# A hybrid decoder step: token tiles transposed by products with a diagonal of row scales, and the first loads reordered

## The chip, the core and the metric

The kernel runs on one core of a Trainium2 chip. The metric is the device time of one execution in microseconds (us), read as the median of the runs shown. TensorE (PE in the profile) multiplies, VectorE (DVE), ScalarE (ACT) and GpSimd (POOL) do the element-wise work, and SyncE (SP) issues most of the DMA transfers. Each engine works through its own list in order and meets the others at semaphores.

## The reference

One step of a decoder layer over 1072 token rows of width 1024: 32 sample tokens, 16 learned meta tokens and 1024 prompt tokens.

```
xn = x * rsqrt(mean(x * x) + eps) * norm_mix          # per token, all float32
z  = xn @ w_in                                        # 1024 -> 3592 columns
...                                                   # short convolutions, gated delta rule with state
h  = x + concat(y_a, y_b) @ w_out
h  = h + relu(rmsnorm(h) @ w_up)^2 @ w_down
y  = rmsnorm(h)                                       # meta tokens dropped from y_prompt
```

Only the first line, and the start of the second, are touched by the change.

## The kernel before

The kernel keeps activations with the features on the 128 partitions and the tokens along the free dimension. x arrives with tokens on the partitions, in nine tiles: tile 0 has 48 rows (samples and meta tokens, `x_small`), tiles 1 to 8 have 128 prompt rows each (`x_big`). The three **groups** of tokens (`GROUPS`) are tiles 0 to 2 (304 columns), tiles 3 to 5 and tiles 6 to 8 (384 columns each). The feature dimension is eight slices k of 128.

A float32 product with enough accuracy is made of three products in a faster type (float32r): high part of the weights by high part of xn, high by low, and low by high. So each 128-column weight tile n of `w_in` is split into `w_h` and `w_l`, and xn into `xh` and `xl`. `dense_part` (lines 1401 to 1403) issues the three products for one slice k of one group. `w_in` has 28 such tiles, and they are followed by `w_out`, `w_up` and `w_down`; TensorE works on them to the end of the kernel.

**How xn is made**, for a tile t:

1. SP loads it (lines 606 to 609 and 742 to 744; semaphores `s_xin`). In SP's list stand tile 0 in two parts, tile 1, tile 2, the first weight tile (line 619), the small block `ab_raw` of eight columns of `w_in` (line 741), tile 3, tiles 4 and 5 in one transfer, tiles 6 to 8 in one transfer. Then SP waits for tiles 4 and 5 and issues seven small loads.
2. ACT squares it and sums along the row (`square_x`, line 1022).
3. DVE makes the mean and adds eps (`mean_x`, line 2035).
4. POOL raises it to the power -1/2 (`x_power`, line 813), which gives `rx`.
5. DVE multiplies the whole tile by `rx` in place (`scale_x`, line 2041, semaphore `x_scaled`).
6. PE transposes the eight slices of it into PSUM banks against the identity `eye` (line 1440 for group 0, `turn_x`, line 1425, for groups 1 and 2). A bank holds one slice k of one group, so it is full when the last tile of the group has been transposed.
7. For each of the 24 pairs m = 8 g + k, ACT writes `xh` from the bank with the factor `tn` (norm_mix, line 1042), and DVE writes `xl` (line 2057).
8. PE waits for `x_low` of m and issues the three products of weight tile 0 (`dense_part(0, ...)`).

PE's list in this part is: the transpose of the norm rows; for each of the tiles 0, 1, 2 first some **idle products** (`IDLE_PRODUCTS`, 3, 1 and 1 of them, line 1431, whose result nobody reads) and then the eight transposes; a wait for `w_low`; the products of m = 0 to 7; `made_ab(0)`, sixteen products with the 16-column `ab_w` (lines 1452 and 1454), which wait for `ab_lo`; the transposes of m = 8 to 11; and then for each m from 8 to 23 the products of m and, five ahead, the transposes of m + 5. At m = 8 it also waits for `ab_kept` and transposes m = 12.

ACT's list is: squares of tiles 0, 1, 2, `split_high(0)` (the high part of weight tile 0, line 1015), the high part of `ab_raw` (line 1035), the square of tile 3, then the 24 evictions with the squares of tiles 4 to 8 between them (`SQUARE_AFTER`: tiles 4, 5, 6 after m = 7, tile 7 after m = 8, tile 8 after m = 10).

DVE's list is: for tiles 0, 1, 2 `mean_x` and `scale_x`; the low part of weight tile 0 (line 2050), `mean_x(3)`, then the 24 `xl` with the other `mean_x` and `scale_x` between them. POOL's list is the nine `x_power` with the low part of `ab_raw` (line 828) after the third. Both the idle products and the wait sit in these lines:

```
for t in GTILES[0]:
    idle_products(IDLE_PRODUCTS[t])
    if t == 0:
        pe.wait_ge(rows_kept, 1)
    pe.wait_ge(x_scaled, t + 1)
```

Of the kernel before, what the change touches and what calls it, by code (L numbers as in the profile page):

```python
# [7 lines left out]
ALU = mybir.AluOpType  # L8
ACT = mybir.ActivationFunctionType
AX = mybir.AxisListType  # L10
F32 = mybir.dt.float32
F32R = mybir.dt.float32r

P = 128
# [10 lines left out]
NT = 1 + SEQ // P  # L25
# [75 lines left out]
def build(nc, x_prompt, x_sample, state_conv_a, state_conv_qkv, state_ssm, meta_tokens, norm_mix, w_in,  # L101
# [4 lines left out]
    with ctx:  # L106
        NY, NSQ = 5, 6

        SLOT = TOK * 4
        R1 = 16512  # L110
        RK = R1 + 16 * SLOT
# [9 lines left out]
        def place(name, shape, dt, offset):  # L121
            return nc.alloc_sbuf_tensor_at(name, shape, dt, offset=offset)
# [10 lines left out]
        def sem(name):  # L133
            return ctx.enter_context(nc.semaphore(name))

        ps_pair = [ctx.enter_context(nc.psum_tensor(f"banks{i}", [P, 2, 512], F32)) for i in range(4)]
        ps = [ps_pair[i // 2][:, i % 2, :] for i in range(8)]
# [16 lines left out]
        w_raw = [place(f"w_raw{i}", [P, KT, P], F32, RING + 4096 * i) for i in range(2)]  # L154
# [7 lines left out]
        x_small = place("x_tok0", [P, D], F32, RZ)  # L162
        square_out = place("square_out", [P, D], F32, RK)
        rows_q = place("rows_q", [28, QKVW], F32, RG)
        rows_a = place("rows_a", [19, CONV], F32, RG + 6144)
        rows_n = place("rows_n", [16, P], F32, RG + 8192)
        ab_raw = place("ab_raw", [P, KT, 8], F32, RG + 3 * SLOT)
# [145 lines left out]
        O_BANK, S_BANK, L_BANK, M_BANK = 4, 5, 6, 7  # L313

        s_norm = sem("s_norm"); s_row = sem("s_row"); s_xin = [sem(f"s_xin{i}") for i in range(6)]; s_const = sem("s_const")
        x_sq = sem("x_sq"); x_pow = sem("x_pow"); x_ms = sem("x_ms"); x_scaled = sem("x_scaled")
        x_turned = sem("x_turned"); x_high = sem("x_high"); x_low = sem("x_low")
        set_ones = sem("set_ones"); rows_turned = sem("rows_turned"); rows_kept = sem("rows_kept")
        ab_hi = sem("ab_hi"); ab_lo = sem("ab_lo"); ab_made = sem("ab_made"); ab_kept = sem("ab_kept")
# [194 lines left out]
        def x_tile(t):  # L514
            return x_small[0:C0, :] if t == 0 else x_big[:, t - 1, :]
# [8 lines left out]

        SQUARE_AFTER = {7: (4, 5, 6), 8: (7,), 10: (8,)}
        AB_AFTER = 9
        IDLE_PRODUCTS = (3, 1, 1)
        TURN_AHEAD = 5

        def turn_bank(g, k):  # L530

            m = KT * g + k
            return k if g == 0 else 3 + (m - KT) % 5

        def rows(t):
            return C0 if t == 0 else P
# [67 lines left out]
        def _(sp):  # L604
# [2 lines left out]
            sp.dma_start(x_small[NS:C0, :], meta_tokens).then_inc(s_xin[0], 16)  # L607
            sp.dma_start(x_big[:, 0:1, :], xp_v[:, 0:1, :]).then_inc(s_xin[1], 16)
            sp.dma_start(x_big[:, 1:2, :], xp_v[:, 1:2, :]).then_inc(s_xin[2], 16)

            def load(n):
                if n >= 2:
# [122 lines left out]
            for n in range(N_IN + 3):  # L735
                if n >= 3:
                    step(3 * (n - 3))
                    step(3 * (n - 3) + 1)
                load(n)
                if n == 0:  # L740
                    sp.dma_start(ab_raw[:, :, :], w_in_v[:, :, O_A:O_A + 8]).then_inc(s_ahead, 16)
                    sp.dma_start(x_big[:, 2:3, :], xp_v[:, 2:3, :]).then_inc(s_xin[3], 16)
                    sp.dma_start(x_big[:, 3:5, :], xp_v[:, 3:5, :]).then_inc(s_xin[4], 16)
                    sp.dma_start(x_big[:, 5:8, :], xp_v[:, 5:8, :]).then_inc(s_xin[5], 16)
                    sp.wait_ge(s_xin[4], 16)
                    sp.dma_start(rows_q[0:24, :], state_conv_qkv.rearrange("l b r c -> (l b r) c")).then_inc(s_row, 16)
                    sp.dma_start(rows_q[24:28, :], conv_qkv_w[0]).then_inc(s_row, 16)
                    sp.dma_start(rows_a[0:16, :], state_conv_a.rearrange("l b r c -> (l b r) c")).then_inc(s_row, 16)
                    sp.dma_start(rows_a[16:19, :], conv_a_w[0]).then_inc(s_row, 16)
                    sp.dma_start(gn[:, :], gdn_norm.rearrange("l (p a) -> (l p) a", a=1)).then_inc(s_row, 16)  # L750
                    sp.dma_start(al[:, :], a_log.to_broadcast([P, NH])).then_inc(s_row, 16)
                    sp.dma_start(dtb[:, :], dt_bias.to_broadcast([P, NH])).then_inc(s_row, 16)
                if n >= 3:
                    step(3 * (n - 3) + 2)
# [50 lines left out]
        def _(pool):  # L805
# [17 lines left out]

            for t in range(NT):
                x_power(t)
                if t == 2:
                    pool.wait_ge(ab_hi, 1)
                    pool.tensor_tensor(ab_w[:, :, 8:16], ab_raw[:, :, :], ab_w[:, :, 0:8].bitcast(F32),
                                       ALU.subtract).then_inc(ab_lo, 1)
# [176 lines left out]
        def _(act):  # L1006
# [3 lines left out]
            def split_high(n):  # L1010

                act.wait_ge(w_load[n % 2], 16 * (n // 2 + 1))
                if n >= 2:
                    act.wait_ge(acc_done, 3 * (n - 1))
                act.activation(w_h[n % 2][:, :, :], w_raw[n % 2][:, :, :], ACT.Copy).then_inc(w_high, 1)  # L1015
# [14 lines left out]

            for t in GTILES[0]:
                square_x(t)
            split_high(0)
            act.wait_ge(s_ahead, 16)
            act.activation(ab_w[:, :, 0:8], ab_raw[:, :, :], ACT.Copy).then_inc(ab_hi, 1)
            square_x(3)
            act.wait_ge(rows_kept, 1)
            for m in range(3 * KT):
                g, k = m // KT, m % KT
                c0, w = GROUPS[g]  # L1040
                act.wait_ge(x_turned, m + 1)
                act.activation(xh[:, k, c0:c0 + w], ps[turn_bank(g, k)][:, 0:w], ACT.Copy,
                               scale=tn[:, k:k + 1]).then_inc(x_high, 1)
                for t in SQUARE_AFTER.get(m, ()):
                    square_x(t)
                if m == AB_AFTER:
                    keep_ab(0)
# [346 lines left out]
        def _(pe):  # L1394
# [21 lines left out]
            def turn_x(m):  # L1416

                g, k = m // KT, m % KT
                c0 = GROUPS[g][0]
                pe.wait_ge(x_low, m - 4 if m >= KT + 5 else m - KT + 4)  # L1420
                for t in GTILES[g]:
                    o, c = tile_cols(t)
                    if k == 0:
                        pe.wait_ge(x_scaled, t + 1)
                    ins = pe.transpose(ps[turn_bank(g, k)][:, o - c0:o - c0 + c], x_tile(t)[:, P * k:P * k + P],
                                       eye[0:c, 0:c])
                ins.then_inc(x_turned, 1)

            def idle_products(count):
# [3 lines left out]
            for t in GTILES[0]:  # L1433
                idle_products(IDLE_PRODUCTS[t])
                if t == 0:
                    pe.wait_ge(rows_kept, 1)
                pe.wait_ge(x_scaled, t + 1)
                o, c = tile_cols(t)
                for k in range(KT):
                    ins = pe.transpose(ps[turn_bank(0, k)][:, o:o + c], x_tile(t)[:, P * k:P * k + P], eye[0:c, 0:c])  # L1440
                    if t == GTILES[0][-1]:
                        ins.then_inc(x_turned, 1)

# [579 lines left out]
        def _(dve):  # L2023
# [8 lines left out]
            def mean_x(t):  # L2032

                dve.wait_ge(x_sq, t + 1)
                dve.tensor_scalar(ssx[0:rows(t), t:t + 1], ssx[0:rows(t), t:t + 1], 1.0 / D, EPS, ALU.mult,
                                  ALU.add).then_inc(x_ms, 1)

            def scale_x(t):

                dve.wait_ge(x_pow, t + 1)  # L2040
                dve.tensor_scalar(x_tile(t), x_tile(t), rx[0:rows(t), t:t + 1], None, ALU.mult).then_inc(x_scaled, 1)

            for t in GTILES[0]:
                mean_x(t)
                if t == 0:
                    dve.wait_ge(rows_turned, 1)
                    dve.tensor_copy(tn[:, :], ps[0][:, 0:16]).then_inc(rows_kept, 1)
                scale_x(t)
            dve.wait_ge(w_high, 1)
            dve.tensor_tensor(w_l[0][:, :, :], w_raw[0][:, :, :], w_h[0][:, :, :].bitcast(F32),  # L2050
                              ALU.subtract).then_inc(w_low, 1)
            mean_x(3)
            for m in range(3 * KT):
                g, k = m // KT, m % KT
                c0, w = GROUPS[g]
                dve.wait_ge(x_high, m + 1)
                dve.scalar_tensor_tensor(out=xl[:, k, c0:c0 + w], in0=ps[turn_bank(g, k)][:, 0:w], scalar=tn[:, k:k + 1],  # L2057
                                         in1=xh[:, k, c0:c0 + w].bitcast(F32), op0=ALU.mult,
                                         op1=ALU.subtract).then_inc(x_low, 1)
                if m == KT - 1:  # L2060
                    scale_x(3)
                    mean_x(4)
                    mean_x(5)
                    scale_x(4)
                    scale_x(5)
                    mean_x(6)
                if m == KT:
                    scale_x(6)
                    mean_x(7)
                if m == KT + 2:  # L2070
                    scale_x(7)
                    mean_x(8)
                if m == KT + 3:
                    scale_x(8)
            dve.wait_ge(rows_turned, 2)
            dve.tensor_copy(tq[:, :, :], ps[3][:, 0:336].rearrange("p (f r) -> p f r", r=28)).then_inc(rows_kept, 1)
            dve.tensor_copy(ta[:, :, :], ps[4][:, 0:76].rearrange("p (f r) -> p f r", r=19)).then_inc(rows_kept, 1)
# [704 lines left out]
```

## Time and profile before

| | us |
|---|---|
| three runs | 1331.97, 1333.32, 1335.27 |
| their median | 1333.32 |
| the profiled execution, its own time | 1332.77 |
| its span, first to last instruction | 1331.0 |
| PE busy with products | 1314.0 (99%) |
| DVE, POOL, ACT busy | 840.4, 524.3, 412.7 |

The span lies inside the execution's own time; 1.8 us are outside it. In the timeline a row gives start, duration, engine, line, operation and how many were merged. PE matmuls are pipelined, so the durations overlap: the pace is the distance between starts. A float32 product shows as two records of PE, a float32r product and a transpose as one. PEld is the load of the stationary operand, which runs beside the products.

### The profile page before, as it was taken

How to read it: one execution, taken by the hardware profiler on the slowest of the kernel's cores; microseconds unless marked ns; L12 is line 12 of the kernel's file. 1: busy time of each engine (PE TensorE's matmuls, PEld its weight loads, DVE VectorE, ACT ScalarE, POOL GpSimd, SP SyncE). 2: the span in 40 equal slices, each digit the busy share in tenths (PEclk: the TensorE clock that was granted, in tenths of full speed). 3: DMA queues.
4: the chain of work that ended last, by engine and by line, in shares of the span. 5: the costliest groups of instructions: out<-in, count | busy, mean ns of one | idle time of the engine just before them, and what ended most of it. 6: DMA issues, size and time to landing. Idle time of an engine off the chain costs nothing.

```text
span 1331.0 us, 22484 instructions
## 1 busy us (share of the span) xinstructions
PE 1314.0 (99%) x8988; PEld 1282.5 (96%) x8988; DVE 840.4 (63%) x1414; ACT 412.7 (31%) x807; POOL 524.3 (39%) x544
## 2 busy tenths in 40 slices
PE   7999999999999999999999999999999999999997
PEld 6899999899999999999999999999999999999997
DVE  6566898436463665556666756756667567566866
ACT  7566652112221213232122222322222223222313
POOL 2322112111111211221367466574574755746811
PEclk9999999999999999999999999999999999999999
DMA  6223553633323323221111212112011121110213
GB/s 193 62 73 91 163 166 80 194 115 88 88 65 82 101 57 90 81 65 48 48 33 48 64 33 63 33 48 64 33 61 51 36 61 48 49 49 32 80 45 118
DMA packets 161947, 99.88 MB, mean 75 GB/s; under 512 B 19736, under 2 KB 156468, under 8 KB 161843
## 3 DMA queue, kind: packets, MB, share of 16 engines
q1 hardware_dynamic: 138866, 85.56, 21.9%
q10 hardware_dynamic: 22976, 12.88, 3.6%
q8 instruction: 72, 1.18, 0.4%
q14 instruction: 33, 0.26, 0.1%
HBM read 77.62 MB, written 20.80 MB: 74 GB/s over the span
## 4 chain that ended last, share of the span: by engine, by line
PE 93%; DVE 3%; ACT 2%; issue 1%; DMA 1%; SPq 0%; POOL 0%; DVEq 0%; ACTq 0%
PE banks L1401 10%; PE banks L1927 9%; PE banks L1403 9%; PE banks L1402 9%; PE banks L1929 9%; PE banks L1928 9%; PE banks L1946 7%; PE banks L1947 7%; PE banks L1945 7%; PE banks L1963 1%; PE banks L1964 1%; PE banks L1965 1%; PE banks L1621 1%; PE banks L1635 1%; PE banks L1857 1%
## 5 line engine op out<-in xcount | busy, mean ns | idle before, releaser
L1927 PE MATMUL banks<-hg_high,w_high 128*128 128x384 f32 (+1 forms) x768 | 249.5, 325 | 0.0
L1929 PE MATMUL banks<-hg_high,w_low 128*128 128x384 f32 (+1 forms) x768 | 247.6, 322 | 0.0
L1928 PE MATMUL banks<-hg_low,w_high 128*128 128x384 f32 (+1 forms) x768 | 247.3, 322 | 0.0
L2674 DVE TENSOR_TENSOR hT<-hT,banks 128x528 f32<-128x528 f32 x280 | 189.4, 701 | 84.0 <-PE banks L1947 76.0
L1401 PE MATMUL banks<-xn_high,w_high 128*128 128x384 f32 (+1 forms) x672 | 226.8, 337 | 0.6 <-DVE xn_low L2057 0.5
L1403 PE MATMUL banks<-xn_high,w_low 128*128 128x384 f32 (+1 forms) x672 | 218.1, 325 | 0.0
L1402 PE MATMUL banks<-xn_low,w_high 128*128 128x384 f32 (+1 forms) x672 | 218.0, 324 | 0.0
L821 POOL TENSOR_TENSOR w_low<-w_raw,w_high 128x1024 fp32r<-128x1024 f32 x31 | 77.0, 2483 | 243.7 <-ACT w_high L1015 243.7
L1927 PEld LDWEIGHTS banks<-hg_high,w_high 128*128 128x128 f32 x768 | 144.2, 188 | 1.9 <-POOL w_low L947 1.7
L1928 PEld LDWEIGHTS banks<-hg_low,w_high 128*128 128x128 f32 x768 | 144.3, 188 | 0.1
L1929 PEld LDWEIGHTS banks<-hg_high,w_low 128*128 128x128 f32 x768 | 144.2, 188 | 0.0
L966 POOL TENSOR_TENSOR w_low<-w_pair,w_high 128x256 fp32r<-128x256 f32 x140 | 104.0, 759 | 66.4 <-ACT w_high L1334 66.4
L2653 DVE TENSOR_TENSOR u_row<-banks,h_squares 128x384 f32<-128x384 f32 (+1 forms) x96 | 50.1, 522 | 126.4 <-PE banks L1929 126.1
L1401 PEld LDWEIGHTS banks<-xn_high,w_high 128*128 128x128 f32 x672 | 126.5, 188 | 3.1 <-DVE xn_low L2057 1.1
L947 POOL TENSOR_TENSOR w_low<-w_raw,w_high 128x1024 fp32r<-128x1024 f32 x31 | 78.3, 2527 | 126.9 <-ACT w_high L1316 120.7
L1947 PE MATMUL banks<-op_high_T,w_low 128*128 128x264 f32 x448 | 127.7, 285 | 0.0
L1946 PE MATMUL banks<-op_low_T,w_high 128*128 128x264 f32 x448 | 127.7, 285 | 0.0
L1945 PE MATMUL banks<-op_high_T,w_high 128*128 128x264 f32 x448 | 127.1, 284 | 0.0
L1402 PEld LDWEIGHTS banks<-xn_low,w_high 128*128 128x128 f32 x672 | 126.7, 189 | 0.0
L1403 PEld LDWEIGHTS banks<-xn_high,w_low 128*128 128x128 f32 x672 | 126.2, 188 | 0.0
L1334 ACT ACTIVATE w_high<-w_pair 128x256 fp32r<-128x256 f32 x140 | 55.4, 415 | 177.6 <-PE banks L1929 84.3
L1947 PE MATMUL banks<-op_high_B,w_low 128*128 128x264 f32 x336 | 95.8, 285 | 0.0
(333 smaller groups left out, 2783.6 us busy)
## 6 DMA issues: line engine op xcount, KB each, us to landing
w_raw<-in_w_up SPq DMA_DIRECT2D x32, 512.0 KB, 4.0
w_pair<-in_w_down SPq DMA_DIRECT2D x32, 512.0 KB, 3.4
w_raw<-in_w_in SPq DMA_DIRECT2D x28, 512.0 KB, 4.3
w_raw<-in_w_out SPq DMA_DIRECT2D x8, 512.0 KB, 4.1
x_slice<-in_x_prompt SPq DMA_DIRECT2D x8, 512.0 KB, 4.2
out<-y_tok SPq DMA_DIRECT2D x8, 512.0 KB, 2.7
v_kept_rows<-v_feat SPq DMA_DIRECT2D x4, 536.0 KB, 2.9
gate_kept_rows<-gate_row SPq DMA_DIRECT2D x4, 536.0 KB, 3.1
```

The source lines that it names most:

```text
L947: pool.tensor_tensor(w_l[half][:, :, :], w_raw[n % 2][:, :, :], w_h[half][:, :, :].bitcast(F32), ALU.subtract).then_inc(w_low, 1)
L966: pool.tensor_tensor(set_of(w_l, b, s), set_source(n, PRODUCTS[x][0]), set_of(w_h, b, s).bitcast(F32), ALU.subtract).then_inc(w_low, 1)
L1401: pe.matmul(bank[:, 0:w], w_h[n % 2][:, k, :], hi[:, c0:c0 + w], start=(k == first), stop=False)
L1402: pe.matmul(bank[:, 0:w], w_h[n % 2][:, k, :], lo[:, c0:c0 + w], start=False, stop=False)
L1403: ins = pe.matmul(bank[:, 0:w], w_l[n % 2][:, k, :], hi[:, c0:c0 + w], start=False, stop=(k == last))
L1927: pe.matmul(bank[:, 0:w], w_h[half][:, k, :], hg_h[:, k, c0:c0 + w], start=(k == 0), stop=False)
L1928: pe.matmul(bank[:, 0:w], w_h[half][:, k, :], hg_l[:, k, c0:c0 + w], start=False, stop=False)
L1929: ins = pe.matmul(bank[:, 0:w], w_l[half][:, k, :], hg_h[:, k, c0:c0 + w], start=False, stop=(k == KT - 1))
L1945: pe.matmul(bank, high[:, j, :], op_h[name][:, j, cols], start=(j == 0), stop=False)
L1946: pe.matmul(bank, high[:, j, :], op_l[name][:, j, cols], start=False, stop=False)
L1947: ins = pe.matmul(bank, low[:, j, :], op_h[name][:, j, cols], start=False, stop=(j == FB // 2 - 1))
L2674: dve.tensor_tensor(hc, hc, both, ALU.add if sign > 0 else ALU.subtract).then_inc(acc_read_dve, 1)
```

## The change

The tiles of x are no longer scaled. For each tile DVE makes instead a diagonal matrix `x_root[t]`, the identity times `rx`, of 48 x 48 or 128 x 128. PE then multiplies each slice of the tile with this matrix, as an ordinary float32 product, where it transposed against `eye` before. The bank holds the same values as before. The load of tile 3 is moved ahead of the first weight tile in SP's list. The high part of weight tile 0 is made by DVE and no longer by ACT. The high part of `ab_raw` moves in ACT's list from before the square of tile 3 to behind the eviction of m = 3, and its low part on POOL from behind the third `x_power` to behind the fourth. `mean_x(3)` moves ahead of the split of weight tile 0. The idle products ahead of tiles 1 and 2 are dropped.

```
+        x_root = [place(f"x_root{t}", [P, P], F32, RK + 16 * SLOT + 4 * P * t) for t in range(NT)]
...
-        IDLE_PRODUCTS = (3, 1, 1)
+        IDLE_PRODUCTS = (3, 0, 0)
...
             sp.dma_start(x_big[:, 1:2, :], xp_v[:, 1:2, :]).then_inc(s_xin[2], 16)
+            sp.dma_start(x_big[:, 2:3, :], xp_v[:, 2:3, :]).then_inc(s_xin[3], 16)
...
                     sp.dma_start(ab_raw[:, :, :], w_in_v[:, :, O_A:O_A + 8]).then_inc(s_ahead, 16)
-                    sp.dma_start(x_big[:, 2:3, :], xp_v[:, 2:3, :]).then_inc(s_xin[3], 16)
...
                 x_power(t)
-                if t == 2:
+                if t == 3:
                     pool.wait_ge(ab_hi, 1)
...
             for t in GTILES[0]:
                 square_x(t)
-            split_high(0)
-            act.wait_ge(s_ahead, 16)
-            act.activation(ab_w[:, :, 0:8], ab_raw[:, :, :], ACT.Copy).then_inc(ab_hi, 1)
             square_x(3)
             act.wait_ge(rows_kept, 1)
             for m in range(3 * KT):
...
+                if m == 3:
+                    act.wait_ge(s_ahead, 16)
+                    act.activation(ab_w[:, :, 0:8], ab_raw[:, :, :], ACT.Copy).then_inc(ab_hi, 1)
...
-                        pe.wait_ge(x_scaled, t + 1)
-                    ins = pe.transpose(ps[turn_bank(g, k)][:, o - c0:o - c0 + c], x_tile(t)[:, P * k:P * k + P],
-                                       eye[0:c, 0:c])
+                        pe.wait_ge(x_rooted, t + 1)
+                    ins = pe.matmul(ps[turn_bank(g, k)][:, o - c0:o - c0 + c], x_tile(t)[:, P * k:P * k + P],
+                                    x_root[t][0:c, 0:c], start=True, stop=True)
...
-                dve.tensor_scalar(x_tile(t), x_tile(t), rx[0:rows(t), t:t + 1], None, ALU.mult).then_inc(x_scaled, 1)
+                dve.tensor_scalar(x_root[t][0:c, 0:c], eye[0:c, 0:c], rx[0:c, t:t + 1], None, ALU.mult).then_inc(x_rooted, 1)
...
-                scale_x(t)
+                root_x(t)
+            mean_x(3)
+            dve.wait_ge(w_load[0], 16)
+            dve.tensor_copy(w_h[0][:, :, :], w_raw[0][:, :, :]).then_inc(w_high, 1)
             dve.wait_ge(w_high, 1)
             dve.tensor_tensor(w_l[0][:, :, :], w_raw[0][:, :, :], w_h[0][:, :, :].bitcast(F32),
                               ALU.subtract).then_inc(w_low, 1)
-            mean_x(3)
```

The transposes of group 0 (line 1440) are replaced in the same way, and the other calls of `scale_x` become `root_x` at the same places.

## Rows read from the trace of the kernel before

**Rows 1.** The page: busy time of the engines, and shares of the chain that ended last.

```profile
PE 1314.0 (99%) x8988; PEld 1282.5 (96%) x8988; DVE 840.4 (63%) x1414; ACT 412.7 (31%) x807; POOL 524.3 (39%) x544
...
PE 93%; DVE 3%; ACT 2%; issue 1%; DMA 1%; SPq 0%; POOL 0%; DVEq 0%; ACTq 0%
```

**Rows 2.** Timeline, PE alone: the end of this part.

```profile
36.03 0.34 PE L1403 MATMUL banks<-xn_high,w_low 128*128 128x384 f32 x1
```

**Rows 3.** Timeline, PE alone: idle products, transposes of group 0, first products.

```profile
5.62 2.45 PE L1431 MATMUL banks<-c_main 128*128 128x208 f32 x6
8.00 1.09 PE L1440 MATMUL banks<-c_main,x_tok 48*128 48x48 f32 x8
9.87 1.91 PE L1440 MATMUL banks<-c_main,x_tok 128*128 128x128 f32 x8
12.27 1.91 PE L1440 MATMUL banks<-c_main,x_tok 128*128 128x128 f32 x8
14.38 0.50 PE L1401 MATMUL banks<-xn_high,w_high 128*128 128x304 f32 x1 [0.20 <-DVE xn_low L2057]
14.72 0.30 PE L1402 MATMUL banks<-xn_low,w_high 128*128 128x304 f32 x1
17.93 1.26 PE L1452 MATMUL banks<-xn_high,ab_w 128*16 128x304 f32 x8
```

**Rows 4.** Timeline: ACT and DVE around the first weights and evictions.

```profile
8.14 1.06 ACT L1022 ACTIVATE square_out<-x_tok 128x1024 f32<-128x1024 f32 x1 [0.85 <-DMA x_tok<-in_x_prompt]
10.09 1.06 ACT L1015 ACTIVATE w_high<-w_raw 128x1024 fp32r<-128x1024 f32 x1 [0.79 <-DMA w_raw<-in_w_in]
11.18 1.23 DVE L2050 TENSOR_TENSOR w_low<-w_raw,w_high 128x1024 fp32r<-128x1024 f32 x1 [0.28 <-ACT w_high L1015]
12.11 1.06 ACT L1022 ACTIVATE square_out<-x_tok 128x1024 f32<-128x1024 f32 x1 [0.82 <-DMA x_tok<-in_x_prompt]
13.17 3.33 ACT L1042 ACTIVATE xn_high<-banks,tn 128x304 fp32r<-128x304 f32 x8
13.70 3.63 DVE L2057 SCALAR_TENSOR_TENSOR xn_low<-banks,tn,xn_high 128x304 fp32r<-128x304 f32 x8 [0.25 <-ACT xn_high L1042]
```

**Rows 5.** Timeline from the end of `made_ab(0)`: PE, and ACT's eviction and `abT`.

```profile
20.14 0.38 PE L1425 MATMUL banks<-c_main,x_tok 128*128 128x128 f32 x2
21.24 0.58 ACT L1042 ACTIVATE xn_high<-banks,tn 128x384 fp32r<-128x384 f32 x1 [0.70 <-PE banks L1425]
22.53 0.44 PE L1401 MATMUL banks<-xn_high,w_high 128*128 128x384 f32 x1 [0.34 <-DVE xn_low L2057]
23.22 0.40 ACT L1029 ACTIVATE abT<-banks 16x304 f32<-16x304 f32 x1
23.67 0.87 PE L1425 MATMUL banks<-c_main,x_tok 128*128 128x128 f32 x6 [0.35 <-ACT abT L1029]
```

**Rows 6.** The chain that ended last, window 0 to 80: one m of its steady part.

```profile
31.52 0.18 PE banks L1403
31.70 0.33 PE banks L1425 x3
```

**Rows 7.** The chain in other windows (100 to 300): groups of four float32 products, 128 columns.

```profile
245.94 1.09 PE banks L1621 x8
281.15 0.89 PE banks L1656 x8
```

**Rows 8.** Groups by line and form, DVE: the nearest rows to what DVE gets.

```profile
L2041 DVE TENSOR_SCALAR x_tok<-x_tok,rx 128x1024 f32<-128x1024 f32 x8 | 6.0, 747 | 1.8 <-POOL rx L813 1.8
L2315 DVE COPY blocks<-inverse 128x1024 f32<-128x1024 f32 x1 | 1.1, 1127 | 0.0
```

**Rows 9.** One stretch of 1 us: busy time (x instructions) by engine, granted clock, DMA share, GB/s.

```profile
10.00:11.00 1.00, 1.00 (x7) 1.00 (x6) 0.75 (x1) 0.92 (x1) 0.11 (x1) 1.00 0.97 389
```

**Rows 10.** Timeline of SP's queue (issue start and duration), and POOL's low part of `ab_raw`.

```profile
3.69 4.41 SPq L742 DMA_DIRECT2D x_tok<-in_x_prompt  x1
14.66 0.37 SPq L746 DMA_DIRECT2D rows_q<-in_state_conv_qkv  x1
...
11.37 1.22 POOL L828 TENSOR_TENSOR ab_w<-ab_raw,ab_w 128x64 fp32r<-128x64 f32 x1 [1.25 <-ACT ab_w L1035]
```

More of the change, by code:

```diff
@@ L315, in build @@
         s_norm = sem("s_norm"); s_row = sem("s_row"); s_xin = [sem(f"s_xin{i}") for i in range(6)]; s_const = sem("s_const")
-        x_sq = sem("x_sq"); x_pow = sem("x_pow"); x_ms = sem("x_ms"); x_scaled = sem("x_scaled")
+        x_sq = sem("x_sq"); x_pow = sem("x_pow"); x_ms = sem("x_ms"); x_rooted = sem("x_rooted")
         x_turned = sem("x_turned"); x_high = sem("x_high"); x_low = sem("x_low")
@@ L1436, in _ @@
                     pe.wait_ge(rows_kept, 1)
-                pe.wait_ge(x_scaled, t + 1)
+                pe.wait_ge(x_rooted, t + 1)
                 o, c = tile_cols(t)
                 for k in range(KT):
-                    ins = pe.transpose(ps[turn_bank(0, k)][:, o:o + c], x_tile(t)[:, P * k:P * k + P], eye[0:c, 0:c])
+                    ins = pe.matmul(ps[turn_bank(0, k)][:, o:o + c], x_tile(t)[:, P * k:P * k + P], x_root[t][0:c, 0:c],
+                                    start=True, stop=True)
                     if t == GTILES[0][-1]:
@@ L2036, in mean_x, with root_x @@
                                   ALU.add).then_inc(x_ms, 1)
-            def scale_x(t):
+            def root_x(t):
+                c = rows(t)
                 dve.wait_ge(x_pow, t + 1)
-                dve.tensor_scalar(x_tile(t), x_tile(t), rx[0:rows(t), t:t + 1], None, ALU.mult).then_inc(x_scaled, 1)
+                dve.tensor_scalar(x_root[t][0:c, 0:c], eye[0:c, 0:c], rx[0:c, t:t + 1], None, ALU.mult).then_inc(x_rooted, 1)
             for t in GTILES[0]:
@@ L2060, in _ @@
                 if m == KT - 1:
-                    scale_x(3)
+                    root_x(3)
                     mean_x(4)
                     mean_x(5)
-                    scale_x(4)
-                    scale_x(5)
+                    root_x(4)
+                    root_x(5)
                     mean_x(6)
                 if m == KT:
-                    scale_x(6)
+                    root_x(6)
                     mean_x(7)
                 if m == KT + 2:
-                    scale_x(7)
+                    root_x(7)
                     mean_x(8)
                 if m == KT + 3:
-                    scale_x(8)
+                    root_x(8)
             dve.wait_ge(rows_turned, 2)
```

## The prediction

> **What bounds the kernel now.** I read the page first. TensorE is busy for 1314.0 of 1331.0 us and holds 93% of the chain that ended last [rows 1]. So work added to PE lengthens the kernel unless it fits into one of PE's waits. The timeline of the first 40 us shows what ends last there. The reader should look for three stretches. Up to 14.38 PE runs idle products and the transposes of group 0 and then waits for the first `xl` [rows 3]. From 14.38 to 20.14 it runs the products of m = 0 to 7 and `made_ab(0)`, closely packed [rows 3, 5]. From 20.14 to about 27.5 it still waits in places, for `xl` and for `abT` among others [rows 5]; from there to 36.37 it never waits, and each m costs three products and three transposes [rows 2, 6]. Behind 36.37 the work on PE is the same in both kernels, so the shift of that moment is the answer.
>
> **PE's added work.** In the steady part three transposes hold 0.33 us of the chain, 0.11 each [rows 6]. A float32 product of the same shape is two records: eight records, which are four products, hold 0.89 [rows 7], 0.223 a product. Each of the 48 turned slices of groups 1 and 2 thus costs 0.112 more, 5.4 us in all. Nothing else of the change lowers PE's work in that stretch.
>
> What of it goes into waits: from 20.14 to 36.37 are 16.2 us. The work in them is 48 transposes at 0.111, 5.3, and the products of m = 8 to 23, 48 at 0.175 (0.18 in the chain's rounding [rows 6]), 8.4, together 13.7. So PE waited 2.5 us. Afterwards the work is 48 x 0.223 + 8.4 = 19.1. The waits go because PE is then later than its suppliers: an m costs it 0.525 + 0.67 = 1.2 us, while an eviction costs ACT or DVE about 0.6. One wait may be left. The turning of m = 12 needs `abT`, and ACT makes that behind the eviction of m = 8, the square of tile 7 and the eviction of m = 9; from the first to the end of `abT` were 2.4 us before, less what it waited between (21.24 to 23.62 [rows 5]). With the turning of m = 8 done at 21.0 that gives 23.4, and with a signal's way 23.5; PE arrives at 20.1 + 12 x 0.223 + 0.525 = 23.3: 0.2 lost. The stretch becomes 19.3 and the change of it **+3.1 us**.
>
> **The start, to 20.14.** Three things must be there before the products of m = 0.
> (1) The weights. The transfer of tile 3 (524 KB) is now ahead of them. At the 389 GB/s of that time [rows 9] it takes 1.35 us, so they land at 10.1 + 1.35 = 11.45; if they and tile 3 simply change places, at 12.1 [rows 4]. DVE's copy is not in the trace. Its neighbours are the scaling of a tile of the same size from SBUF, 0.747, and a copy of the same size with turned strides, 1.127 [rows 8]. I take 0.75, since both sides are contiguous as in the scaling, and keep 1.13 for the range. The low part is 1.23 [rows 4]. That makes 11.45 + 0.75 + 1.25 = 13.45 for `w_low`, and DVE starts `xl` of m = 0 at 13.5 where it started at 13.70. Bounds: 13.2 (weights 0.3 earlier) to 14.6 (12.1, slow copy).
> (2) The banks. `x_high` started at 13.17 because ACT was still squaring tile 3, which landed at 12.1 [rows 4]. Now tile 3 follows tile 2, whose square began at 8.14 [rows 4], by 1.35; ACT is free at 10.8 and follows PE. The scaling of 0.75 becomes a 128 x 128 one; between a tiny one of about 0.15 and 0.747 [rows 8] I take 0.2, a gain of 0.5 for each tile, but PE, not DVE, is last here.
> (3) PE's own list. It is ready for tile 0 at 8.0 as before [rows 3]. The transposes of tiles 1 and 2 go at (1.91 - 0.42) / 7 = 0.213 a record [rows 3], twice the 0.111 of later [rows 6]. The granted clock reads 1.00 here too [rows 9], yet this pace is that of 1.2 GHz and the later one that of 2.4 GHz; the fast pace sets in at 14.7, right after the first weight product [rows 3]. The products take for tile 0 sixteen records at 0.11, 1.8 us (0.9 before), and for tiles 1 and 2 sixteen each: 3.4 us a tile at the slow pace, 1.8 at the fast one. Dropped are two idle products, 1.4 us. With the slow pace for tile 1 and the fast one for tile 2 the list is done at 8.0 + 1.8 + 3.4 + 1.8 = 15.0; with the fast pace from the middle of tile 1 at 14.1.
> The products of m = 0 to 7 then end at 18.3 in the first case (15.0 + 8 x 0.42) and at 17.6 in the second, where DVE's pace of 0.45 an m from 13.5 binds; 17.93 before [rows 3]. I take **0** for the start, with -0.4 and +2.3 as ends.
>
> The Trainium skill ("TensorE: Matmul & The Clock Gate", PE-mode transpose) says that transposes do not count as TensorE work for releasing its clock. By that rule the root products, which are ordinary ones, would bring the fast pace earlier than transposes did. The trace agrees as far as it goes: the slow pace outlasts 24 transposes. The sum stays the same by it, since `w_low` binds then; by the rule alone the first rival would have a smaller chance than the rows give it.
>
> **What is moved.** On SP the weights and `ab_raw` are issued one issue of 0.44 later. The issue that stood for 4.41 us, as behind a full queue [rows 10], will be that of `ab_raw` or of tiles 4 and 5; those landed at 14.6, where SP goes on [rows 10], and ACT takes them up behind m = 7, after 16.3, so 1.7 us cover it. The seven small loads behind are read after 36 [rows 2]. On ACT 1.06 for the weights goes, and the high part of `ab_raw` (0.24) comes behind m = 3, about 14.5; the evictions behind it run ahead of DVE's `xl`, so it costs nothing. On POOL the low part (1.22 [rows 10]) then ends at about 16.0. `made_ab(0)` waits for it at 17.9, and queued behind it is the power of tile 4, which wants a square that ACT makes only behind m = 7, after 17: over 1 us of cover for both. On DVE the split now waits for the weights with the 24 `xl` queued behind it; that is in (1). From m = 8 on the root steps take 0.5 less each than the scalings, on an engine that is no longer last there: nothing.
>
> **Sum.** 0 + 3.1 = +3.1 us. The profiled execution took 1332.77, so 1335.9 against its own time; the median of the three runs, 1333.32, is 0.55 higher, so 1336.4 beside it, or +0.23%. What a measurement of this kernel can tell from no change is about 0.3%, 4 us, so this counts as no change, close to the border.
>
> **Rivals.**
> *The clock stays slow through tiles 1 and 2* (slower). Both tiles take 3.4 us, so PE is done with tile 2 at 8.0 + 1.8 + 6.8 = 16.6, the products of m = 0 to 7 end at 20.1, 2.2 later than before, and the total is +5.3, 1338.6. For it: about 9 us of idle products and transposes did not bring the fast pace before. Against it: PE now runs products without a gap from 5.6 on, where it had transposes between. It decides slower once the slow pace reaches 1 us into tile 2's work. Chance 0.16.
> *Each bunch of products pays for a held weight load* (slower). Eight records behind a wait held 1.09 instead of 0.89 in one place [rows 7]. The 16 bunches of `turn_x` each stand behind a wait; 16 x 0.2 = 3.2 more, +6.3 in all, 1339.6. Against it: the transposes have the same waits and show no such loss [rows 6]. Chance 0.06.
> *The weights come late* (no change or slower). Landing at 12.1 and a copy of 1.13: `xl` starts 0.9 later than before, total +4.0, 1337.3. Chance 0.10.
> *A product with the root matrix costs a transpose's time.* Then the change doesn't add PE work, the scalings leave DVE, and half of PE's 2.5 us of waits and a little of the start are won: -1.5, 1331.8. Against it stand all float32 products of the trace. Chance 0.08.
> *Forecast*, its own range 1335.3 to 1337.5: chance 0.60.
>
> **Chances.** Slower by over 0.3%: 0.16 + 0.06 + half of 0.10 + about a tenth of the forecast's 0.60 (its upper end lies at the border), 0.33. Faster: a part of the last rival, 0.03. The rest, 0.64, is no change. The range takes in the forecast, the late weights and the slow clock, and above it half a microsecond for the spread of runs: up to 1339.2. Below it reaches to no change at all, 1333.3, where half of what the last rival wins is met. Left out are the second rival and the lower half of the last, about 0.1.
>
> **What would show it.** Right: the last three-product row of m = 23 near 39.5 instead of 36.0; the rows of the turning twice as many and 0.67 us for each three; no waits of PE behind 24; the first products of weight tile 0 near 14.2 to 15. Wrong: turning records at 0.21 apart for tile 2 (first rival), more than 1.3 us from one m to the next (second), DVE's low part of the weights ending after 14 (third), one record for each turned slice (fourth). The forecast falls as a whole if the span changes by less than 1.5 or more than 5 us.

## The result and the profile after

| | before | after |
|---|---|---|
| median of six runs each, us | 1333.17 | 1340.81 |
| lowest and highest of the changed kernel | | 1338.61, 1342.40 |
| ratio, 95% interval | | 1.0050 [1.0039, 1.0061] |
| profiled execution, its own time | 1332.77 | 1342.40 |
| its span | 1331.0 | 1340.6 |

The changed kernel is slower by 0.50%, 6.7 us (1333.2 x 0.0050). The forecast was +3.1 us, 1336.4, and the range ended at 1339.2: the sign was right and the size under half. The whole interval lies above the 0.3% up to which the prediction counted a shift as no change (0.64 of its chances); this is the case to which it gave 0.33. The page of the kernel after, busy time and shares of the chain, answers to [rows 1]:

```profile
PE 1324.5 (99%) x9056; PEld 1295.2 (97%) x9056; DVE 835.9 (62%) x1415; ACT 412.4 (31%) x806; POOL 523.8 (39%) x544
...
PE 95%; DVE 3%; ACT 1%; issue 1%; DMA 0%; ACTq 0%; DVEq 0%
```

PE gained work, DVE and ACT lost a little, and PE's share of the chain rose. The next view is the timeline of PE alone in the kernel after, from its first instruction to the end of m = 23; it answers to [rows 2, 3, 5].

```profile
6.32 0.25 PE L1411 MATMUL banks<-c_main,rows_n 16*128 16x16 f32 x1 [6.32 <-DMA rows_n<-in_norm_ffn]
6.50 2.45 PE L1432 MATMUL banks<-c_main 128*128 128x208 f32 x6
8.88 9.84 PE L1441 MATMUL banks<-x_root,x_tok 48*128 48x48 f32 x48
18.47 0.38 PE L1402 MATMUL banks<-xn_high,w_high 128*128 128x304 f32 x1
...
21.88 1.27 PE L1454 MATMUL banks<-xn_high,ab_w 128*16 128x304 f32 x8
...
24.10 2.84 PE L1426 MATMUL banks<-x_root,x_tok 128*128 128x128 f32 x24
...
43.23 0.34 PE L1404 MATMUL banks<-xn_high,w_low 128*128 128x384 f32 x1
```

The reader is to see one unbroken row of 48 root records where before there were three bunches of eight transposes with idle products between [rows 3], and two shifts:

| stretch | before | after | difference |
|---|---|---|---|
| start of the turning of tile 0 | 8.00 | 8.88 | +0.9 |
| from there to the first weight product | 6.38 | 9.59 | +3.2 |
| m = 0 to 7 | 3.55 | 3.41 | -0.1 |
| `made_ab(0)` | 2.21 | 2.22 | 0 |
| from there to the last product of m = 23 | 15.89 | 19.13 | +3.2 |
| last product of m = 23 | 36.03 | 43.23 | +7.2 |

The first 0.9 belongs to the execution, not to the change: PE's first instruction waits for a load (`rows_n`), and in the three runs below that have the same load order it starts at 4.80 to 4.97. So 6.3 us are the change's own.

How the start spends its time, in the groups by form of PE between 8.8 and 17.3 in the kernel after, then between 7.9 and 14.3 in the kernel before:

```profile
L1441 PE MATMUL banks<-x_root,x_tok 128*128 128x128 f32 x22 | 5.1, 428 | 0.0
L1441 PE MATMUL banks<-x_root,x_tok 48*128 48x48 f32 x16 | 3.6, 412 | 0.0
```

```profile
L1440 PE MATMUL banks<-c_main,x_tok 128*128 128x128 f32 x16 | 3.8, 421 | 0.0
...
L1440 PE MATMUL banks<-c_main,x_tok 48*128 48x48 f32 x8 | 1.1, 308 | 0.0
```

Durations overlap, so the price of a transpose is read from its starts: the last seven transposes of tile 0 start between 8.14 and 8.78 in the kernel before, 0.11 us apart, half of the 0.21 of a large tile. A root record of tile 0 took 3.6 / 16 = 0.22, the same as one of a large tile (5.1 / 22 = 0.23; from start to start both are 0.21). Sixteen records at 0.22 are 3.5 us, not the 1.8 of the forecast. Windows over the same row, of line L1441 alone (busy PE with its records, busy PEld, granted clock, DMA share, GB/s):

```profile
8.80:12.40 3.60, 3.52 (x16) 3.49 (x16) 1.00 1.16 297
12.40:15.40 3.00, 3.00 (x15) 2.95 (x15) 1.00 1.02 399
17.00:17.50 0.50, 0.50 (x4) 0.50 (x4) 1.00 1.02 406
17.50:18.00 0.50, 0.50 (x7) 0.50 (x6) 1.00 1.10 226
```

A window also counts a record that reaches over its edge. Four records in half a microsecond are the slow pace, seven the fast one: it comes only at 17.5, when tile 2 is half done. The granted clock reads 1.00 throughout, as it did before at this pace [rows 9], so in these records the start's level has to be read from the pace.

What ACT and DVE did in the meantime, in the timelines of ACT and DVE, answering to [rows 4]:

```profile
16.76 1.73 ACT L1040 ACTIVATE xn_high<-banks,tn 128x304 fp32r<-128x304 f32 x4 [6.00 <-PE banks L1441]
...
11.77 0.69 DVE L2054 CAST w_high<-w_raw 128x1024 fp32r<-128x1024 f32 x1 [0.82 <-DMA w_raw<-in_w_in]
12.49 1.23 DVE L2056 TENSOR_TENSOR w_low<-w_raw,w_high 128x1024 fp32r<-128x1024 f32 x1
17.30 3.63 DVE L2062 SCALAR_TENSOR_TENSOR xn_low<-banks,tn,xn_high 128x304 fp32r<-128x304 f32 x8 [3.58 <-ACT xn_high L1040]
```

ACT stood idle for 6.00 us and DVE for 3.58, both behind PE. The weights were split by 13.7, near the 13.45 of the forecast, and nobody waited for them. The steady part, one m of the chain that ended last and the start of the next (start, duration, what), answers to [rows 6]:

```profile
31.91 0.67 PE banks L1426 x6
32.58 0.18 PE banks L1402
32.76 0.17 PE banks L1403
32.93 0.18 PE banks L1404
33.11 0.67 PE banks L1426 x6
```

An m costs 33.11 - 31.91 = 1.20 us without a wait, as forecast (0.525 + 0.67).

Behind 43.23 the work is the same, and there one thing differs between executions: stretches at half clock. Windows of PE alone, first the kernel after, then before (busy time with records, granted clock, DMA share, GB/s):

```profile
65.00:69.00 4.00, 4.00 (x20) 0.57 0.04 12
249.00:253.50 4.50, 4.50 (x22) 0.62 0.46 137
```

```profile
65.00:69.00 4.00, 4.00 (x25) 1.00 0.49 131
249.00:253.50 4.50, 4.50 (x20) 1.00 0.39 118
```

A granted clock of 0.57 over 4 us is 3.4 us at half speed; so is 0.62 over 4.5. For work that is bound by the clock alone such a stretch would cost half of that, 1.7 us. What it did cost can be read behind the last product of m = 23: the rest of the span is 1294.3 and 1295.0 us in the profiled executions without one (e1 below, and before), 1295.8 to 1296.3 in those with one (e3, e4, e8) and 1297.3 to 1297.5 in those with two (after, e2, e5, e6, e7), so 1.2 to 1.5 us each. The two profiles differ by 9.6 us: 7.2 up to m = 23 and 2.4 behind it, where the medians differ by 7.6 and the paired ratio says 6.7.

The kernel before has such stretches in other runs: the mean granted clock runs from 0.995 to 0.998 in the changed kernel's runs and from 0.995 to 0.999 in the 62 runs of the kernel before whose clocks are on record. The changed kernel's run at 0.998 has a span of 1336.8, and the seventeen of the kernel before at 0.998 have a mean of 1330.8: 6.0 apart, near the 6.3 of the table above. Whether the change makes the stretches more frequent is open: four of its six runs are at 0.995, and eight of the 62.

### The profile page after: what moved, and what is told of

The parts are those of the page before. It is cut to its first block, busy times and chain, and to the rows that moved or that the text cites. A ratio compares the mean times of both kernels' runs of the same rounds, so it can differ in the third digit from the quotient of the medians.

```text
span 1340.6 us, 22620 instructions
## 1 busy us (share of the span) xinstructions
PE 1324.5 (99%) x9056; PEld 1295.2 (97%) x9056; DVE 835.9 (62%) x1415; ACT 412.4 (31%) x806; POOL 523.8 (39%) x544
## 4 chain that ended last, share of the span: by engine, by line
PE 95%; DVE 3%; ACT 1%; issue 1%; DMA 0%; ACTq 0%; DVEq 0%
PE banks L1402 10%; PE banks L1404 9%; PE banks L1403 9%; PE banks L1929 9%; PE banks L1931 9%; PE banks L1930 9%; PE banks L1948 7%; PE banks L1949 7%; PE banks L1947 7%; PE banks L1965 1%; PE banks L1966 1%; PE banks L1967 1%; PE banks L1623 1%; PE banks L1637 1%; PE banks L1426 1%
```

## The experiments

Eight kernels ran, in two sets of four, each against the kernel before on the same chip. **A** says that the time is PE's own added work, in group 0 and in groups 1 and 2; **B** that the moved load or the moved steps cost something; **C** that the half clock of the start doubles what the root products of group 0 cost.

| kernel | first weight product | last product of m = 23 | ratio to before, 95% interval |
|---|---|---|---|
| before | 14.38 | 36.03 | 1 |
| after | 18.47 | 43.23 | 1.0050 [1.0039, 1.0061] |
| e1, roots in group 0 alone | 17.10 | 38.28 | 1.0023 [1.0014, 1.0032] |
| e2, roots in groups 1 and 2 alone | 13.70 | 38.56 | 1.0021 [1.0012, 1.0030] |
| e3, no roots, the rest of the change | 14.00 | 35.81 | 1.0001 [0.9992, 1.0010] |
| e4, after, with dense products first | 14.34 | 39.21 | 1.0013 [1.0004, 1.0022] |
| e5, before, with dense products first | 13.44 | 35.06 | 1.0003 [0.9993, 1.0012] |
| e6, after, with the old load order | 16.40 | 41.27 | 1.0041 [1.0028, 1.0054] |
| e7, e3 with dense products first | 13.30 | 34.41 | 0.9996 [0.9986, 1.0005] |
| e8, e5 with a square moved | 12.49 | 34.90 | 0.9992 [0.9984, 1.0001] |

### One part at a time: e1, e2, e3

e1 keeps the root products of group 0 and turns groups 1 and 2 with transposes again, whose tiles DVE scales as before:

```
-  ins = pe.matmul(ps[turn_bank(g, k)][:, ...], x_tile(t)[:, ...], x_root[t][0:c, 0:c], start=True, stop=True)
+  ins = pe.transpose(ps[turn_bank(g, k)][:, ...], x_tile(t)[:, ...], eye[0:c, 0:c])
...
+  if t >= 3: dve.tensor_scalar(x_tile(t), x_tile(t), rx[0:c, t:t + 1], None, ALU.mult)
```

> The changed kernel with the tiles of groups 1 and 2 scaled and transposed as before (48 transposes in place of 48 root products); group 0, the loads and the split as changed. Theory A (PE's own work): each turned slice of groups 1 and 2 is one record of 0.11 us instead of two, 5.3 us less work of which 2 come back as waits, so about 3.2 us faster than the changed kernel, some 3.5 to 4 slower than the kernel before; the products of m = 0 start where they start in the changed kernel, 18.5. Theory B (the start alone, the load order and what hangs on it, makes the loss): no faster than the changed kernel by more than 1 us.

e2 is the reverse:

```
-  IDLE_PRODUCTS = (3, 0, 0)
+  IDLE_PRODUCTS = (3, 1, 1)
...
-  ins = pe.matmul(ps[turn_bank(0, k)][:, o:o + c], x_tile(t)[:, ...], x_root[t][0:c, 0:c],
+  ins = pe.transpose(ps[turn_bank(0, k)][:, o:o + c], x_tile(t)[:, ...], eye[0:c, 0:c])
...
+  if t < 3: dve.tensor_scalar(x_tile(t), x_tile(t), rx[0:c, t:t + 1], None, ALU.mult)
```

> The changed kernel with group 0 scaled and transposed as before, and the idle products back at 3, 1, 1; groups 1 and 2 with root products, loads and split as changed. Theory A: PE's list ahead of the first weight product shortens by the 24 doubled slices, 3.2 us, so the first weight product starts near 15.2 (14.4 plus 0.9 for the late first transfer) and the kernel is about 3.2 us faster than the changed one. Theory B (load order): the first weight product stays behind 17.5 and the gain is under 1 us. The row of m = 23's last product then stands near 40.

e3 makes both edits, so that of the change only the load order, the split on DVE and the moved steps (both parts of `ab_raw`, `mean_x(3)`) are left. The idle products ahead of tiles 1 and 2 go with group 0 in these edits; no run separates dropping them from the root products of that group.

> The changed kernel with all nine tiles scaled and transposed as before and the idle products at 3, 1, 1: what is left is the load order, DVE's high part of the weights and the moved parts of the small block. Theory A: within 1 us of the kernel before, 0.9 of it from the constants that land later (first PE instruction at 6.3 instead of 5.4). If the two root parts add up, its gain over the changed kernel is the sum of those of the two kernels that restore one part each, about 6.4 us. Theory B: still 3 us or more slower than the kernel before.

Measured: 1337.71, 1337.60 and 1335.06 beside 1334.59 of the kernel before. The parts are +0.23%, +0.21% and +0.01%, together 0.45% against 0.50% of the whole change; the intervals allow full additivity. The moves alone cost nothing (**B** falls), and each of the two sets of root products costs about 3 us (**A** stands). Inside the executions, from the first start of tile 0 to the last product of m = 23, it adds up as well: 28.0 us before, 30.9 in e1 (+2.8), 31.0 in e2 (+3.0), 28.2 in e3 (+0.2) and 34.4 after (+6.3). The stamps came 1.4 to 1.5 us sooner than expected in e1 and e2, since their expectations counted the changed kernel's late first load as a part of the load order. It is not: e1, e2 and e3 have that order and start at 4.85, 4.80 and 4.97. e1's timeline of PE has the same unbroken row as the changed kernel, 9.9 us of it, though it began 1.5 us sooner:

```profile
4.85 0.26 PE L1411 MATMUL banks<-c_main,rows_n 16*128 16x16 f32 x1 [4.85 <-DMA rows_n<-in_norm_ffn]
...
7.41 9.94 PE L1441 MATMUL banks<-x_root,x_tok 48*128 48x48 f32 x48
17.10 0.39 PE L1402 MATMUL banks<-xn_high,w_high 128*128 128x304 f32 x1
```

In e2 transposes and root products meet in one timeline of PE: in group 0 the transposes of tiles 0, 1 and 2, then the turning of m = 8 to 11.

```profile
4.80 0.25 PE L1411 MATMUL banks<-c_main,rows_n 16*128 16x16 f32 x1 [4.80 <-DMA rows_n<-in_norm_ffn]
...
7.57 1.06 PE L1441 MATMUL banks<-c_main,x_tok 48*128 48x48 f32 x8
...
9.50 1.97 PE L1441 MATMUL banks<-c_main,x_tok 128*128 128x128 f32 x8
...
11.95 1.32 PE L1441 MATMUL banks<-c_main,x_tok 128*128 128x128 f32 x8
...
19.43 2.84 PE L1426 MATMUL banks<-x_root,x_tok 128*128 128x128 f32 x24
```

Tile 2's eight transposes hold 1.32, against 1.97 for tile 1: here the fast pace came at about 12.5, early in tile 2 and 7.7 us after PE's first instruction, with nothing but transposes and idle products ahead of it. With root products it came after 11.2 us in the changed kernel (17.5 - 6.3), 11.4 in e1 (16.3, from where the starts of its records come 0.11 apart, less 4.85) and 9.8 in e6 below (14.7 - 4.93), with transposes after 9.3 in the kernel before (14.7 - 5.4) and 9.7 in e3. Root products did not bring it earlier than transposes. The Trainium skill ("TensorE: Matmul & The Clock Gate", PE-mode transpose) says that transposes do not count for releasing the clock. By that rule the root products should have brought the fast pace earlier, and in these few executions they did not; the rule itself is not tested, since idle products, which are ordinary ones, stand among the transposes. Why the slow pace outlasted some 40 root records without a gap stays open.

### The clock of the start: e4 and e5

Nine 512-column products on a tile of ones that nobody reads stand ahead of PE's first product; e4 has them in the changed kernel, e5 in the kernel before:

```
+  pool.memset(warm[:, :].bitcast(F32), 1.0).then_inc(set_ones, 1)
...
+  pe.wait_ge(set_ones, 1)
+  for _ in range(9):
+      pe.matmul(ps[7][:, 0:512], warm[:, 0:P], warm[:, 0:512], start=True, stop=True)
```

> The changed kernel with nine dense products of 512 columns on a constant tile put on PE ahead of its first wait (about 1.5 to 5.5 us, when PE was idle), nothing else. Theory C (the slow pace of the start is the clock's lower level, which PE's earlier work decides): the 48 records of group 0 go 0.11 apart instead of 0.213 and take 5.3 us instead of 9.6, the first weight product starts near 14.6 and the kernel is 3 to 4 us faster than the changed one. Rival D (the pace of 0.213 belongs to float32 products and transposes that start cold from DMA-fed tiles, whatever PE did before): the records stay 0.213 apart and the time does not change by more than 0.5 us.

> The kernel before with nine dense 512-column products ahead of its first product and nothing else changed. Theory A (the change lost time to TensorE's own work at half clock; the first stage of the kernel before has slack on TensorE, since ScalarE's first eviction waited for ScalarE's own list until 13.17): the start gains little, first weight product at 13.9 to 14.4 against 14.38, time 1333.5 to 1334.6 (0 to -0.8 us against the kernel before), so that the warm-up which was worth 4 us to the changed kernel is worth under 1 us here, and the changed kernel with it stays behind this one by about 2 to 3 us. Rival E (the half clock costs every kernel's start the same): the same 4 us gain here, 1330.5. A gain between 1.5 and 3 would say that the slack on TensorE is smaller than the chain shows.

Measured: 1336.37 (e4). Against the changed kernel 0.50% became 0.13%: 4.9 us came back (0.0037 x 1333; by the ends of the two intervals 2.3 to 7.6), where 3 to 4 were expected. By the stamp of m = 23, 3.2 us of loss are left (39.21 less 36.03), the price of groups 1 and 2; the ratio says 1.7, and its interval ends at 2.9. The timeline of PE in e4:

```profile
1.31 4.21 PE L1413 MATMUL banks<-warm 128*128 128x512 f32 x9 [1.31 <-POOL minus_half L810]
5.86 0.20 PE L1416 MATMUL banks<-c_main,rows_n 16*128 16x16 f32 x1 [0.34 <-DMA rows_n<-in_norm_ffn]
5.99 1.32 PE L1437 MATMUL banks<-c_main 128*128 128x208 f32 x6
7.24 7.34 PE L1446 MATMUL banks<-x_root,x_tok 48*128 48x48 f32 x48
14.34 0.38 PE L1404 MATMUL banks<-xn_high,w_high 128*128 128x304 f32 x1
```

The six idle products take 1.32 instead of 2.45 [rows 3]. The windows of the root row in e4 (columns as above) show both levels in one row, and here the granted clock tells them apart:

```profile
7.20:9.00 1.80, 1.76 (x15) 1.76 (x16) 0.95 1.03 365
9.00:12.00 3.00, 3.00 (x15) 2.91 (x15) 0.50 0.99 256
12.00:14.40 2.40, 2.40 (x22) 2.39 (x21) 0.95 1.03 420
```

At the fast level a record of the 48-row tile takes 0.12 (1.80 / 15) and one of a large tile 0.11; at half clock it is 0.20. So a root record's price halves with the clock and does not depend on whether the tile has 48 or 128 columns: **C** stands, and tile 0's 3.5 us is explained. PE did stay dense between 9 and 12, yet the clock fell back for that time, so the row took 7.34 and not the 5.3 expected. In e5 and e8, which have transposes there and PE busy for 2.5 and 2.6 of the same 3 us, it did not fall. Why is not settled, and whether more dense work would hold it was not tried.

e5: 1334.68, against 1333.77 for the kernel before in its set; no gain. Its first weight product comes 0.9 sooner than before, 13.44, twice what was expected of it at most, since the square of tile 3 on ACT also happened to begin 0.9 sooner (its DMA was done earlier in this execution). The timeline of ACT in e5 shows what the first eviction waits for, a square and not PE:

```profile
11.17 1.06 ACT L1024 ACTIVATE square_out<-x_tok 128x1024 f32<-128x1024 f32 x1 [0.21 <-DMA x_tok<-in_x_prompt]
...
12.23 3.33 ACT L1044 ACTIVATE xn_high<-banks,tn 128x304 fp32r<-128x304 f32 x8
```

The rival that the half clock costs every kernel alike (1330.5) falls. With transposes the half clock is hidden behind ACT's list but for about 1 us; with root products nothing hides it. That the earlier end of m = 23 (35.06) does not show in the median goes with more time at half clock in e5's runs: five of its twelve have a mean granted clock of 0.994, which no run of the kernel before has. At equal mean clock (0.995, 0.996, 0.997, 0.998) e5's mean span is shorter than that of the kernel before in its set by 0.6, 1.6, 1.0 and 1.8 us, from few runs each. Whether the dense products bring the extra time at half clock is open.

### The load order with root products: e6

```
-  sp.dma_start(x_big[:, 2:3, :], xp_v[:, 2:3, :])        # ahead of load(0)
...
+  sp.dma_start(x_big[:, 2:3, :], xp_v[:, 2:3, :])        # behind ab_raw, as before
```

> The changed kernel with the load of the third large tile put back behind the weights and ab_raw; root products everywhere. Theory A (TensorE's own work): 1340 +- 1.5 like the changed kernel, root products of the start at 0.21 us per record until about 17, first weight product 18 to 18.7. Rival B (the moved load costs something of its own): 1337.5 or less, with the first weight product 1.5 us or more sooner than 18.47.

Measured: 1339.83 against 1333.77, ratio 1.0041, which overlaps the changed kernel's. **A** is right on the time: **B** wanted 1337.5 or less. The stamps missed: the first weight product came at 16.40, not 18 to 18.7. PE's first instruction was early (4.93 where the changed kernel's was at 6.32), and from the start of tile 0 the root row took 8.90 instead of 9.59, since the fast pace came at 14.7, 7.2 us after that start, where the changed kernel had it after 8.6 (17.5 - 8.88). A stamp of one execution shifts by more than the median does; differences inside an execution are what can be compared.

### Is there a version that beats both: e7 and e8

e7 is e3 with the dense products. e8 is e5 with the square of tile 3 off ACT's path to the first eviction:

```
-  square_x(3)                    # ahead of ACT's eviction loop
+  if m == 3: square_x(3)         # in it, behind the eviction of m = 3
...
-  mean_x(3)                      # ahead of DVE's xl loop
+  if m == 4: mean_x(3)           # in it, behind xl of m = 4
```

> Transposes everywhere with the new load order and VectorE's high part (the run without roots) and the nine dense products ahead. VectorE's chain there: tile 2 scaled at 11.2, high part to 11.95, low part to 13.2, first low part of x at 13.3 to 13.8. Theory A with VectorE as the bound of that start: first weight product 13.7 to 14.0, time 1334.3 to 1335.2, 0 to -0.6 us against the run without roots. If TensorE at half clock was still the bound there: first weight product 13.2, and 1 us less time.

> The kernel before with the nine dense products ahead, and with the square of the third large tile moved on ScalarE behind the eviction of m=3 (its mean on VectorE behind m=4). With both covers of the first eviction gone (ScalarE's square until 13.1, TensorE's half clock) it starts at about 12.2 instead of 13.17: first weight product 13.2 to 13.5, time 1333.2 to 1333.8 against about 1334.6 of the kernel before (-0.8 to -1.4 us). If only one of the two bounds the start, it equals the run with the dense products alone.

Measured: 1333.52 (e7) and 1333.08 (e8) against 1333.77. e7 did better than expected: its first weight product came at 13.30, not 13.7 to 14.0, and still behind a wait of 1.63 us for DVE, whose low part of the weights began 0.5 us sooner than in e3 (11.48 against 11.97). It also gives the pair for e4: with the dense products the changed kernel is 0.17% slower than its version without root products (1.0013 and 0.9996, from two sets), 2.3 us, and without them 0.49%, 6.5 us. e8's first weight product came sooner than its 13.2 to 13.5 too. ACT's timeline in e8:

```profile
10.55 0.24 ACT L1037 ACTIVATE ab_w<-ab_raw 128x64 fp32r<-128x64 f32 x1
10.98 1.73 ACT L1043 ACTIVATE xn_high<-banks,tn 128x304 fp32r<-128x304 f32 x4 [0.20 <-PE banks L1446]
12.59 1.07 ACT L1024 ACTIVATE square_out<-x_tok 128x1024 f32<-128x1024 f32 x1
```

With both covers gone the first eviction starts at 10.98, and the first weight product at 12.49, 1.9 us sooner than before. But the square now sits between two evictions, PE waits for `xl` of m = 4, and by the end of m = 23 only 1.1 us are left (34.90). The ratio is 0.9992 with an interval that reaches 1.0001: the estimate, -1.1 us (0.0008 x 1334), fits the expectation, but this many runs do not show it to be a gain. Neither version is shown to be faster than the kernel before; both beat the changed kernel.

## Why the prediction was wrong

- **PE's added work in groups 1 and 2**: right. The forecast was +3.1; measured are +3.24 in the stretch 20.14 to 36.03 of before against 24.10 to 43.23 of after, +2.8 us in e2's time (0.0021 x 1334). The 0.223 for a root product was right (0.67 for three), and so was the 1.20 of an m. The 0.2 of waiting for `abT` did not come: the stretch took 19.13, not 19.3.
- **The start**: wrong, and the failing step is (3), "PE's own list". "The products take for tile 0 sixteen records at 0.11, 1.8 us" took the pace of tile 0's transposes for the price of a root record. Measured: 0.22 a record, 3.5 us, so +1.7. At the half clock a transpose of the 48-row tile took half of a large tile's time; a float32 record of the same tile took as much as a large tile's. The second half of the step, the fast pace for all of tile 2, gave 1.8 where it took about 2.7 (eight records at 0.21, eight at 0.11, and a little to the first weight product): +0.9. And "I take **0** for the start" chose between +0.4 of the sum and -0.4: another 0.4. Together 3.0 of the 3.1 that the start really cost (17.93 to 21.88 less 0.88).
- **The range's end of +2.3** took in the slow clock and the late weights, but no row for tile 0's records; that is why it missed. A float32 product on a 48-row tile had no row in the trace of before, and should have had the price of the large tile's record as its upper bound.
- **First rival** (the clock stays slow through tiles 1 and 2): half right. The slow pace lasted 1.7 us into tile 2, past the 1 us that the rival set as its sign. Its +5.3 fell short because it too had tile 0 at 1.8; its end of the products of m = 0 to 7 is 20.0 by its own terms (16.6 + 8 x 0.42), not 20.1.
- **Held weight loads, late weights, a product at a transpose's price**: none happened. The total of the second rival, +6.3, is the nearest in number to what was measured, by luck alone: an m costs 1.20 and not more than 1.3, the low part of the weights was done at 13.7, and two records stand for each turned slice.
- **The moved steps**: right at nothing (e3, 1.0001). SP's long issue fell on `ab_raw` (2.57 us) and on tiles 4 and 5 (3.14 us), and its queue reached the small loads at 14.48, as foreseen (14.66 before [rows 10]). The low part of `ab_raw` on POOL ended at 19.0, ahead of `made_ab(0)` at 21.88.
- **The steps on DVE**: the split's copy took 0.69 (0.75 priced), a root matrix 0.24 to 0.29 (0.2 priced). The gain of 0.5 a tile reached nobody, as PE was last.
- **The prediction's own signs**: the last row of m = 23 was to stand near 39.5 and the first weight products near 14.2 to 15; they stood at 43.23 and 18.47. The forecast was to fall as a whole beyond 5 us of span, and 9.6 were measured.
- **The remainder** between 6.3 us of stage and 6.7 (paired) to 7.6 (medians) is within what the half-clock stretches of single executions make.

## What to carry over

A multiplication that is folded into a transpose is not free on TensorE: the transpose was one record, the float32 product is two, and the price is paid on the engine that holds 93% of the chain, to relieve one that had slack. In this kernel PE's first ten microseconds and more go at the half-clock pace: price them so, take an unseen shape at the larger of its neighbours' prices, and ask which other engine's list hides PE's slow start before the change and no longer does behind it. In a kernel of 1.3 ms a shift of 0.5% must be read from stretches inside an execution, with the granted clock beside each run.

## What the runs showed of the hardware

- At half clock a float32 record on a 48-row, 48-column tile took 0.22 us, as long as on a 128 x 128 tile; a transpose of the small tile took 0.11 from start to start, of the large one 0.21. At full clock the float32 records took 0.12 and 0.11.
- The fast pace set in 7.7 to 11.4 us after PE's first instruction, whether transposes or root products ran, and in the latter case with no wait of PE from 6.50 on in the changed kernel. Nine dense 512-column products from 1.31 on had it there by 5.99 in e4, but in e8, with the same products, the six idle products still took 2.18 us and the fast pace came at about 7.5. In e4 it was lost again from 9 to 12 with PE busy throughout.
- Single stretches of about 3.4 us at half clock fall where PE is busy throughout, at 65 and 249 us in the changed kernel's profile and in e4 at 9 and 60 us. Behind m = 23 each made the rest of the span 1.2 to 1.5 us longer. The profile of the kernel before has none ahead of its last 6 us, though its other runs have mean granted clocks as low.
- These stretches come at two places of the work and not at any: one begins 20.8 to 22.1 us behind the last product of m = 23 (after 65.4, e2 60.3, e4 60.0, e5 57.1, e6 62.5, e7 56.0), the other 204.1 to 206.4 us behind it (after 249.7, e2 244.6, e3 239.9, e5 241.4, e6 246.8, e7 240.3, e8 239.6). Some executions have both, some one, and e1 and the kernel before neither; what brings them is open.
- The granted clock reads 1.00 in the first slow microseconds where no fall preceded them, and 0.50 where one did.
